# A two-layer encoder trunk: first weights on ScalarE's queue, smaller release steps, a moved scatter and a shared final norm

## The reference

```python
for layer in range(2):
    h = rmsnorm(x, norm_mix[layer])
    x = x + (even_mixer, odd_mixer)[layer](h)       # in-projection, heads, out-projection
    h = rmsnorm(x, norm_ffn[layer])
    x = x + hierarchical_moe(h)                     # 32 experts, 2 of them for each token
return rmsnorm(x, norm_final)

def hierarchical_moe(h, ...):
    for e in range(32):
        hid = silu(h @ w_gate[e]) * (h @ w_up[e])   # w_gate, w_up: 1024 x 512
        y = y + gates[e] * (hid @ w_down[e])        # w_down: 512 x 1024
```

## Time and profile before

| | |
|---|---|
| median of three runs | 1184.88 us (1184.63 to 1184.89) |
| profiled execution, its own time | 1186.47 us |
| its span, first to last instruction | 1184.7 us |
| TensorE matmul busy | 998.1 us, 84% |
| DVE, ACT busy | 276.8 us, 130.1 us |
| DMA | 442.43 MB, mean 373 GB/s |
| mean granted TensorE clock | 0.932 of 2.4 GHz |

### The profile page before, as it was taken

The page is one execution under the profiler, slowest core; times in us unless marked ns, Lnnn a source line. Parts: engine busy times, 40 slices in busy tenths (PEclk is TensorE's granted clock), DMA queues, the critical chain, the costliest instruction groups (busy, mean ns, idle before and its releaser), DMA issues.

```text
span 1184.7 us, 12720 instructions
## 1 busy us (share of the span) xinstructions
PE 998.1 (84%) x5268; PEld 457.9 (39%) x5268; DVE 276.8 (23%) x653; ACT 130.1 (11%) x309; POOL 3.5 (0%) x10
## 2 busy tenths in 40 slices
PE   8999999967767768977999999999677777779776
PEld 7675553313213213342485555533132132233422
DVE  1265352202102101110322453512011011012103
ACT  2024020000000000000231120200000000000001
POOL 0000000000000000000000000000000000000000
PEclk9999999989879879988999999999898798799889
DMA  9923989999999999999973518999999999999996
GB/s 365 411 77 133 418 329 425 428 427 428 427 430 427 428 429 427 426 426 423 412 327 142 213 71 340 352 428 426 426 430 427 428 429 426 429 427 428 425 422 249
DMA packets 39297, 442.43 MB, mean 373 GB/s; under 512 B 4386, under 2 KB 4770, under 8 KB 12484
## 3 DMA queue, kind: packets, MB, share of 16 engines
q1 hardware_dynamic: 39092, 441.47, 89.4%
q10 hardware_dynamic: 144, 0.13, 0.0%
HBM read 440.54 MB, written 1.05 MB: 373 GB/s over the span
## 4 chain that ended last, share of the span: by engine, by line
PE 52%; DMA 42%; issue 3%; DVE 1%; SPq 1%; ACT 0%; POOL 0%; DVEq 0%; POOLq 0%
PE psum L1707 51%; DMA sb_weights<-moe_w_down 38%; DMA sb_weights<-moe_w_gate 3%; SPq L668 1%; DMA sb_weights<-moe_w_up 1%; DMA sb_weights<-ev_w_in_units 1%; PE psum L2302 0%; DVE sb_weights L1578 0%; DVE sb_x L1598 0%; PE psum L1885 0%; PE psum L1745 0%; PE psum L2170 0%; PE psum L2080 0%; PE psum L1983 0%; ACT sb_weights L914 0%
## 5 line engine op out<-in xcount | busy, mean ns | idle before, releaser
L1707 PE MATMUL psum<-sb_weights,sb_hT 128*32 128x512 f32 (+3 forms) x2368 | 469.4, 629 | 102.9 <-DMA sb_weights<-moe_w_gate 59.8
L1707 PE MATMUL psum<-sb_weights 128*32 128x512 f32 (+12 forms) x1632 | 319.8, 561 | 43.5 <-DMA sb_weights<-moe_w_down 38.7
L1707 PEld LDWEIGHTS psum<-sb_weights,sb_hT 128*32 128x32 f32 (+2 forms) x2368 | 148.2, 128 | 396.0 <-issue 315.7
L1707 PEld LDWEIGHTS psum<-sb_weights 128*32 128x32 f32 (+7 forms) x1632 | 116.2, 139 | 235.2 <-issue 192.1
L1591 DVE TENSOR_TENSOR sb_x<-sb_x,psum 128x512 f32<-128x512 f32 x84 | 57.7, 687 | 281.6 <-PE psum L1707 281.6
L1707 PE MATMUL psum<-sb_hT,sb_weights 128*128 128x256 f32 (+1 forms) x400 | 88.8, 380 | 0.9 <-DMA sb_weights<-ev_w_in_units 0.8
L1707 PEld LDWEIGHTS psum<-sb_hT,sb_weights 128*128 128x128 f32 (+1 forms) x400 | 74.0, 187 | 13.5 <-issue 1.6
L1707 PE MATMUL psum<-sb_weights,sb_hn 128*128 128x192 f32 (+2 forms) x448 | 72.2, 321 | 6.4 <-issue 6.2
L1707 PEld LDWEIGHTS psum<-sb_weights,sb_hn 128*128 128x128 f32 x448 | 69.3, 204 | 11.1 <-issue 11.1
L1583 DVE COPY sb_weights<-psum 96x512 f32<-96x512 f32 (+1 forms) x20 | 13.7, 687 | 180.6 <-PE psum L1707 180.6
L1578 DVE TENSOR_TENSOR sb_weights<-sb_weights,psum 96x512 f32<-96x512 f32 (+1 forms) x22 | 15.0, 684 | 159.5 <-PE psum L1707 159.4
(11 more groups left out here) (201 smaller groups left out, 340.7 us busy)
## 6 DMA issues: line engine op xcount, KB each, us to landing
sb_weights<-moe_w_gate SPq DMA_DIRECT2D x60, 2048.0 KB, 24.5
sb_weights<-moe_w_down SPq DMA_DIRECT2D x58, 2048.0 KB, 27.1
sb_weights<-moe_w_up SPq DMA_DIRECT2D x50, 2048.0 KB, 27.1
sb_weights<-moe_w_up SPq DMA_DIRECT2D x18, 1024.0 KB, 23.2
sb_weights<-od_w_in_units SPq DMA_DIRECT2D x6, 2048.0 KB, 27.4
sb_weights<-ev_w_in_units SPq DMA_DIRECT2D x5, 2048.0 KB, 25.5
sb_weights<-moe_w_up SPq DMA_DIRECT2D x20, 512.0 KB, 8.5
sb_weights<-moe_w_gate SPq DMA_DIRECT2D x16, 512.0 KB, 7.1
```

The source lines that it names most:

```text
L1707: return nc.tensor.matmul(o, l, r, start=start, stop=stop, skip_group_check=True)
```

## The change

1. **First weights.** The two 512 KB pieces of unit 0 are issued by ACT right behind `lead`, and no longer by SP. SP goes from x straight to the rest of unit 0.
2. **Eighths.** In `expand_first` the first gate matmuls (j = 0) release `quarter_used` once more, and SP loads the first half of the first quarter of two experts (256 KB each) on that, in both layers. The other half follows on the old release.
3. **Turns.** `turn_mix` is hooked in one block earlier, `turn_o1` of the last head too. `project1(11, 1)` is cut in two, with `chunk_kv(3, 1)` between its halves.
4. **Routing.** The first half of tile 1's logits and the turn of its last quarter go ahead of tile 0's ranks on TensorE; on DVE the copy of that quarter and the inverse root go ahead of the ranks.
5. **Last round.** The scatter of the round before goes ahead of gate, followed by two matmuls of 512 columns of the identity; four more stand between the turn of the hidden values and the wait for its copy.
6. **Final norm.** DVE multiplies the first halves by the gain as soon as they are added (`final_gain`), ACT scales them by the inverse root and stores them itself; DVE and SP do only the second halves. The squares of the first halves are written to PSUM.

```diff
@@ mixer_weights (SP), and the start of ACT's program @@
-                    at = 0
-                    if layer == 0 and c == 0:
-                        for b in range(2):
-                            sp.dma_start(unit[c][:, at:at + D], w_ins[layer][c][:, at:at + D]
-                                         ).then_inc(first_full[b], 16)
-                            at += D
+                    at = 2 * D if layer == c == 0 else 0
             act.dma_start(lead[:, 0:PARAMS + P], A["lead"]).then_inc(lead_loaded, 16)
+            for b in range(2):
+                cols = slice(b * D, (b + 1) * D)
+                act.dma_start(unit[0][:, cols], w_ins[0][0][:, cols]).then_inc(first_full[b], 16)
@@ second_round (SP) and expand_first (TensorE) @@
+                sp.wait_ge(quarter_used, 4 * layer + 1)
+                for k in range(1, LIGHT):
...
+                    sp.dma_start(unit[SLOT["gate"] + k][:, 0:HALF], src[:, 0:HALF]).then_inc(held_full, 16)
...
+                        begin = HALF if part == 0 and kind == "gate" else part * 2 * HALF
+                        rows = slice(begin, (part + 1) * 2 * HALF)
...
+                                if j == 0 and kind == "gate" and frees:
+                                    ins.then_inc(quarter_used, 1)
@@ residual (DVE) @@
-                ranked(layer, 0)
-                nc.vector.tensor_tensor(light_sel[:, 0], light_iota[:, 0], light_shape(rt_R, 0)[:, 0], ALU.is_equal
-                                        ).then_inc(main.early_sel, 1)
                 turned_quarter(1)
                 inverse_root(n, 1)
+                ranked(layer, 0)
+                nc.vector.tensor_tensor(light_sel[:, 0], light_iota[:, 0], light_shape(rt_R, 0)[:, 0], ALU.is_equal
+                                        ).then_inc(main.early_sel, 1)
@@ mixer1 (TensorE) @@
                 chunk_kv(3, 0)
-                project1(11, 1)
+                project1(11, 1, 0)
                 chunk_kv(3, 1)
+                project1(11, 1, 1)
                 chunk_kv(3, 2)
...
-                            6, lambda: turn_o1(C_HEADS - 1))
+                            5, lambda: turn_o1(C_HEADS - 1))
@@ expert_round (TensorE) @@
+                if columns:
+                    scatter(s, n - 1, 1 - h, 0)
+                    scatter(s, n - 1, 1 - h, 1)
+                    keep_warm(HALF, HALF, bank=4)
                 if first:
                     expand_first()
                 else:
                     expand("gate", 0)
-                if prior:
+                if prior and not columns:
...
+                if columns:
+                    keep_warm(HALF, HALF, HALF, HALF, bank=3)
                 pe.wait_ge(s.hidT_done, n + 1)
@@ the end (DVE, ACT, SP) @@
+            def final_gain(t):
+
+                nc.vector.tensor_tensor(y[:, t, 0:HALF], x[:, t, 0:HALF], gfin[:, 0:HALF], ALU.mult)
...
+            for t in range(TILES):
+                i = TILES * 4 + t
+                act.wait_ge(inv_done, i + 1 - TILES * 2)
+                nc.scalar.activation(y[:, t, 0:HALF], y[:, t, 0:HALF], ACT.Copy, scale=rrms[:, i:i + 1]
+                                     ).then_inc(late_scaled, 1)
+            for t in range(TILES):
+                act.wait_ge(late_scaled, 2 + t + 1)
+                act.dma_start(out[0, t * P:(t + 1) * P, 0:HALF], y[:, t, 0:HALF]).then_inc(out_stored, 16)
```

More of the change, by code:

```diff
@@ L696, in _ @@
             for t in range(TILES):
[L697 to L700, removed]
+                sp.wait_ge(x_done, t + 1)
+                sp.dma_start(out[0, t * P:(t + 1) * P, HALF:D], y[:, t, HALF:D]).then_inc(out_stored, 16)
             sp.wait_ge(out_stored, 16 * TILES * 2)
@@ L1659, in final_rounds @@
                     return
-                add_round(s, r + 1, (0, 1))
+                if layer:
+                    dve.wait_ge(gfin_done, 2)
+                for t in range(TILES):
+                    add_round(s, r + 1, (t,))
+                    if layer:
+                        dve.wait_ge(s.x_added, (r + 1) * 4 + t + 5)
+                        final_gain(t)
                 dve.wait_ge(s.used["down"], r + 2)
@@ L1697, in _ @@
                     gains(1)
-            dve.wait_ge(gfin_done, 2)
             for t in range(TILES):
-                inverse(4, t)
+                mean_square(4, t)
+            for t in range(TILES):
+                inverse_root(4, t)
                 final_norm(t)
@@ L1784, in column_tokens, with project @@
                 return hTc[:, j, i * P:(i + 1) * P]
-            def project(layer, c, i, group, step, by_token, free=None):
+            def project(layer, c, i, group, step, by_token, free=None, part=None):
                 if c == layer == i == 0:
@@ L1797, in project @@
                     w = unit[c].rearrange("p (j n) -> p j n", j=KT)
-                    for j in range(4 * step, 4 * step + 4):
+                    js = range(4 * step, 4 * step + 4)
+                    for j in js if part is None else js[2 * part:2 * part + 2]:
                         ins = mm(psum[:, group % 2], by_token(j, i), w[:, j, :], j == 0, j == KT - 1)
@@ L1806, in project @@
                                  j == 0, j == KT - 1)
-                if step == 1:
+                if step == 1 and part != 0:
                     ins.then_inc(proj_psum, 1)
@@ L1961, in project1 @@
                         free = (sg_done, g - 9)
-                    project(1, c, g % 2, g, step, None if c in COL_UNITS[1] else plain_tokens, free)
+                    project(1, c, g % 2, g, step, None if c in COL_UNITS[1] else plain_tokens, free, part)
                 def gates(c):
@@ L2090, in route @@
                     pe.wait_ge(cst_loaded, 2 * 16)
+                logits(layer, 1, 0)
+                turn_quarter(layer, 1)
                 pe.wait_ge(mask_done, TILES * layer + 1)
```

31 lines of the change are left out of this document (15 added, 16 removed).

## The result

The changed kernel takes 1187.22 us (median of 8 runs, 1185.68 to 1190.4); the kernel before, run beside it, 1184.99 us (8 runs, 1184.63 to 1186.41). The ratio is 1.0019, 95% interval 1.001 to 1.0028. So it is 2.2 us slower, where 2.5 us faster was forecast. The difference is small, 0.2%, but its interval doesn't reach 1. The profiled execution took 1187.56 us with a span of 1185.8, 1.1 us above that of before.

A forecast was written before the change was run, and what follows sets the result against it. Weight arrival was taken to bound the MoE layers, TensorE the mixers and seams. The terms 0.7 - 1.2 - 0.9 - 0.5 - 1.8 + 2.6 - 1.4 = -2.5 us gave 1182.4 us from 1184.88, range 1178.8 to 1185.6.

The forecast's parts named there:

- first weights: Kernel start: weights issued 0.5 us earlier but sharing the queues' hardware, so +0.7 us, bounds -0.9 and +2.0.
- small moves: Mixers and routing: turns -0.4 and -0.8, halved product -0.9, routing -0.3 and -0.2 us, by covering idles.
- eighths: First expert round of both layers: SP issues 0.9 us earlier, so -0.9 us each, -1.8 together; other bound 0.
- last rounds: Last expert round of each layer: +1.9 us in layer 1 and +0.7 in layer 0, +2.6 in the sum.
- final norm: Kernel end: tiles shared by DVE and ACT, last store issued at about 1180.8, -1.4 us, between -1.0 and -1.8.
- A microsecond earlier there is a microsecond earlier for the rest of the layer: First expert round: an earlier restart of the weight stream at SP's first load carries through the layer.
- Point (3): Sign: SP's first second-round load 1.5 to 2.5 us earlier from projection's start (layer 0), 2.5 to 3 from mixer's (layer 1).
- the rival of the releases that don't arrive: Restart too slow for earlier loads: eighths and routing give nothing, +2.3 us on the sum, 1184.7 us; chance 0.20.
- point (2): Sign: no idle over 0.2 us at the three TensorE idles at the turns and before the recurrence's last step.
- point (1): Sign at the kernel's start: the first projection starts between 9.2 and 10 us, not before 9.
- the hole: Last round, middle of up: TensorE idles 3.9 us for up's second half, then some 3.2 us at the low clock.
- a long low clock: Rival: low clock from up's second half into down's first product, 1189.3 us with 10 us per layer; chance 0.09.

The follow-up runs named there:

- a3: The changed kernel with the eighths undone, gate's quarter released whole as before: 1187.35 us, ratio 1.0021 to the kernel before.
- c2: The changed kernel with last rounds, first weights and eighths undone: 1183.08 us, ratio 0.9978 to the kernel before.
- c1: The changed kernel with last rounds and first weights undone, the rest kept: 1182.02 us, ratio 0.9976 to the kernel before.
- a1: The changed kernel with the last rounds undone (scatter behind gate, no extra matmuls): 1184.08 us, ratio 0.9989 to the kernel before.
- a2: The changed kernel with the first weights on SP's queue again: 1186.08 us, ratio 1.0008 to the kernel before.
- c4: The kernel before with only the first weights moved to ACT's queue: 1186.12 us, ratio 1.0009.
- d2: The changed kernel with first weights undone and, of the last-round edits, only the four extra matmuls behind up: 1186.47 us, ratio 1.0001 to the kernel before.
- d1: The changed kernel with first weights undone and, of the last-round edits, only scatter and its two matmuls before gate: 1184.9 us, ratio 0.9986 to the kernel before.
- b3: The changed kernel with first weights undone, scatter within up, five extra matmuls before gate, without the four: 1184.06 us, ratio 0.9998 to the kernel before.

## Why the prediction was wrong

The account from the runs, in us, with the forecast behind it: first weights +0.9 to +2.1 (+0.7), small moves -1.5 (-2.6 with routing), eighths -0.1 to -1.1 (-1.8), last rounds +3.1 to +4.1 (+2.6), final norm -0.6 to -1.5 (-1.4). Each is uncertain by about 1 us. For the eighths the ratios of both pairs, a3 and the changed kernel, c2 and c1, give 0.2 us faster, the medians 0.1 and 1.1.

- **Eighths: the step that failed.** "A microsecond earlier there is a microsecond earlier for the rest of the layer" took SP's first issue for the bound. I had read that TensorE waits 0.17 us for up at 750.72 and called the sides nearly even; that wait was the bound. The eighths moved the first 0.5 MB by 1.1 to 1.2 us. All later quarters are released by TensorE behind up's last unit, so at 50 and at 267 MB the lead is gone (the table at c2). Point (3) of the forecast came true, in layer 0 even with more than I said (2.9 us earlier counted from the projection's start, of which 1.5 was the low clock in the trace of before), and was worth nothing that could be told from no change. This is the rival of the releases that don't arrive, by another mechanism than I gave it: not a slow restart, but the later releases, which wait for a transfer that the edit doesn't touch.
- **Small moves.** The three idles of the earlier trace rows are gone, as point (2) asked, and the mixer of layer 1 gains 1.6 us from its start to the release of the arena. What I missed is that up's last unit binds the first round. It is issued behind the output product and landed 9.5 to 10.8 us later; with the new order TensorE asks for it after 9.2 (gate's start at 7.3 and 1.92 for its quarter). So routing's 0.4 us became wait, and all 14 versions with the small moves wait for it in both layers, 0.3 to 1.6 us. In layer 0 the trace of before hid this: its low clock in the routing made TensorE 1.5 us late, and the unit had landed when it asked. What the turns and the halved product gain in mixer 1 reaches SP's issue of the unit and so the stream.
- **First weights.** Sign and size were right, for half the reason. The first piece of the weights, which I had put 0.7 us later, landed 0.4 us earlier than before (8.6 against 9.0 us); the second landed at 13.0 in place of 10.2, about when TensorE comes to it, and a1 waited another 1.35 us for weights at 15.8. What held up the start is x: the projection began at 9.74, as point (1) has it, but x's second piece had lost its place to the weights (TensorE begins on it at 7.4 to 7.6 us in all eight profiled executions with this edit, in the eight without it had landed by 6.3 to 6.7), and in five of the eight with it TensorE turned it at the low clock (12 products in 2.6 to 2.8 us); in the other eleven the full clock was there for at least nine of the twelve products. The Trainium skill (DMA: Bandwidth & Descriptors, Issuing engines are not separate DMA queues) says that queues of different engines run on the same hardware; the trace agrees, and a2 and c4 put the price at 1 us.
- **Last rounds.** Forecast well: gate 7.07 us, the hole 3.84 and 3.74 us against 3.9, the low level 3.4 us against 3.2, layer 1 +2.2 against +1.9. Layer 0 took 1.3 from gate's start to the next projection, against 0.7. What I got wrong was calling the hole the loss and the four a detail: alone they cost 4.4 us (d2), the order alone 2.9 (d1), and both together no more than the four.
- **Final norm.** The last store was issued no later than forecast, but four stores within 1.2 us land 0.7 us later each than four spread over 3.1 us. I had priced the issue and not the landing.

The chances: slower had 0.07, mostly for a long low clock, and none of it came so. For the range's upper end, 1185.6, the prediction has no sum; two terms that I held for safe (eighths, small moves) were off by 2.9 us together.

## What to carry to other kernels

Before releasing a buffer earlier, look at which transfer the engine waits for just behind it. If the following releases hang on that transfer, the early start moves only its own rows (here 0.5 MB), and a few MB on the lead is gone. Compare such a place in several executions: a low clock in one trace hid the wait here, and a scatter of 1 us in one landing looked like an effect. Filler matmuls pay only inside a wait that exists: count their time against the idle in the row (here 3.63 us against 0.58), and look whether work that is moved forward leaves a longer idle at the place it came from. At the start the second issuing engine bought nothing here: the first weights came 0.4 us earlier, and x's second piece 0.9 and the second weights 2.8 us later.

## What the runs showed of the hardware

- In the executions with the first weights on ACT's queue the second piece of x landed 6.1 to 6.4 us after its issue, in the others 5.1 to 5.5, and in five of eight the products after it ran at half speed up to 10 to 13 us (in four of the five the record of the granted clock begins only there, and the lengths of the products tell it); in the eight executions without, the full clock was reached by 7.1 us. At the low level the projection began at 9.7 to 10.2 us, in the other three at 8.8 to 8.9. The wait before those products was 1.0 to 1.1 us in seven of the eight (0.4 or less without the edit), and both levels followed it.
- An idle of 3.83 us in d1 was followed by the low level twice, 6.83 us from 1154.88 and again 3.41 us from 1165.12, with the full clock between; one of 3.74 us in the changed kernel by 3.41 us once. The length behind a like hole isn't fixed.
- The last 2 MB unit of up in the first round landed 9.5 to 10.8 us after its issue in 16 profiled executions, and 9.7 to 10.7 in layer 0 of five executions (a2, b3, c1, d1, d2) of programs that are the same up to there.
- Four stores of 256 KB that leave within 1.2 us from two queues land 2.8 to 2.9 us after issue; from one queue, spread over 3.1 us, 2.1.
